# Final layer norm of a decoder step: three of nine row tiles by VectorE statistics, a ScalarE scaling pass and GpSimd products

## What is computed

```python
def layer_norm(x, g, b):
    xf = x.astype(jnp.float32)
    mu = xf.mean(-1, keepdims=True)
    var = jnp.square(xf - mu).mean(-1, keepdims=True)
    return ((xf - mu) * lax.rsqrt(var + LN_EPS) * g + b).astype(x.dtype)
...
yp = layer_norm(ALPHA * yp + moe(yp, w_router, b_router, w1[l], w3[l], w2[l]), ln2_g[l], ln2_b[l])
ys = layer_norm(ALPHA * ys + moe(ys, w_router, b_router, w1[l], w3[l], w2[l]), ln2_g[l], ln2_b[l])
```

## Time and profile before

| | us |
|---|---|
| median of 3 runs | 1405.29 (1403.64 to 1407.12) |
| the profiled execution, its own time | 1407.36 |
| its span, first to last instruction | 1405.37 |
| TensorE / VectorE / ScalarE / GpSimd busy in the span | 1286.0 / 882.7 / 577.1 / 224.2 |
| mean granted TensorE clock | 0.965 |

### The profile page before, as it was taken

How to read it: one execution, slowest core, us unless ns; L and a number is a source line. 1 busy time by engine, 2 the same in 40 slices (tenths; PEclk the granted TensorE clock), 3 DMA queues, 4 the chain that set the end, 5 groups by cost and what they waited for, 6 DMA issues and landing times.

```text
span 1405.4 us, 20304 instructions
## 1 busy us (share of the span) xinstructions
PE 1286.0 (92%) x7862; PEld 1088.6 (77%) x7862; DVE 882.7 (63%) x1416; ACT 577.1 (41%) x892; POOL 224.2 (16%) x213
## 2 busy tenths in 40 slices
PE   6999999998999999999999999999649999999940
PEld 4788667774699999999889999777538778888830
DVE  3574454434557777665332445557868899999936
ACT  3452564325621111112111111212327888888837
POOL 0200000006022212410210000000472111122130
PEclk9999999999999999999999999999759999999975
DMA  8123301002056655654563512423778999997736
GB/s 242 56 88 108 129 1 40 21 5 86 8 191 198 212 173 174 201 192 169 173 245 98 210 68 87 146 66 91 287 293 310 379 300 339 313 318 248 254 79 241
DMA packets 75428, 240.24 MB, mean 171 GB/s; under 512 B 17093, under 2 KB 27556, under 8 KB 61502
## 3 DMA queue, kind: packets, MB, share of 16 engines
q1 hardware_dynamic: 48598, 160.80, 32.3%
q0 software_dynamic: 18032, 61.31, 14.7%
q10 hardware_dynamic: 8704, 16.84, 3.4%
HBM read 215.65 MB, written 65.76 MB: 200 GB/s over the span
## 4 chain that ended last, share of the span: by engine, by line
PE 79%; DVE 4%; ACT 4%; DMA 4%; issue 2%; POOL 0%; SPq 0%; POOLq 0%; DVEq 0%; ACTq 0%
PE ps L536 19%; PE ps L538 18%; PE ps L537 18%; PE ps L1543 5%; PE ps L1567 3%; PE ps L1568 3%; PE ps L1569 3%; PE ps L1674 3%; PE ps L1714 2%; DMA b<-in_w 2%; PE ps L578 1%; DMA tmp_yd<-b,b 1%; ACT b L966 1%; ACT b L962 1%; ACT b L883 1%
## 5 line engine op out<-in xcount | busy, mean ns | idle before, releaser
L536 PE MATMUL ps<-b,b 128*128 128x344 f32 (+2 forms) x1488 | 525.6, 353 | 3.9 <-issue 2.0
L538 PE MATMUL ps<-b,b 128*128 128x344 f32 (+2 forms) x1488 | 515.6, 347 | 0.0
L537 PE MATMUL ps<-b,b 128*128 128x344 f32 (+2 forms) x1488 | 515.6, 346 | 0.0
L536 PEld LDWEIGHTS ps<-b,b 128*128 128x128 f32 (+1 forms) x1488 | 279.3, 188 | 37.7 <-issue 11.9
L538 PEld LDWEIGHTS ps<-b,b 128*128 128x128 f32 (+1 forms) x1488 | 278.9, 187 | 24.7
L537 PEld LDWEIGHTS ps<-b,b 128*128 128x128 f32 (+1 forms) x1488 | 279.2, 188 | 21.3
L813 ACT ACTIVATE b<-ps,b 128x344 f32<-128x344 f32 x96 | 52.7, 549 | 391.6 <-PE ps L538 391.6
L1315 DVE TENSOR_TENSOR b<-b,b 128x2048 fp32r<-128x2048 f32 x64 | 146.5, 2291 | 18.5 <-ACT b L883 16.4
L1543 PE MATMUL ps<-b,b 128*128 128x128 f32 (+1 forms) x782 | 116.0, 281 | 35.2 <-DMA b<-tmp_xs 18.3
L1104 DVE TENSOR_TENSOR b<-b,ps 128x344 f32<-128x344 f32 x72 | 36.9, 512 | 176.3 <-PE ps L538 169.8
L1543 PEld LDWEIGHTS ps<-b,b 128*128 128x128 f32 (+1 forms) x782 | 91.3, 144 | 60.6 <-DMA b<-tmp_xs 18.4
(11 more groups left out here) (289 smaller groups left out, 1500.5 us busy)
## 6 DMA issues: line engine op xcount, KB each, us to landing
b<-in_w SPq DMA_DIRECT2D x96, 1024.0 KB
b<-in_w_merge SPq DMA_DIRECT2D x32, 640.5 KB, 4.5
tmp_xs<-b ACTq DMA_DIRECT2D x32, 514.0 KB, 4.4
b<-tmp_xs SPq DMA_DIRECT2D x32, 514.0 KB
b<-in_w_in SPq DMA_DIRECT2D x8, 1024.0 KB, 7.5
b<-in_xT SPq DMA_DIRECT2D x4, 1024.0 KB, 11.9
b<-in_w_out SPq DMA_DIRECT2D x4, 1024.0 KB, 8.0
b<-in_x SPq DMA_DIRECT2D x8, 512.0 KB, 4.1
```

The source lines that it names most:

```text
L536: mm(out, hi, mhi, start=start, stop=False)
L537: mm(out, hi, mlo, start=False, stop=False)
L538: return mm(out, lo, mhi, start=False, stop=stop)
```

## The change

Slots 1, 3 and 5 go another way. VectorE takes their mean and variance with `bn_stats` and `bn_aggr` (`moments`), ScalarE takes the root (`root`), VectorE forms the reciprocal and minus mean times reciprocal (`shift`), ScalarE makes one pass z * reciprocal + shift in place (`scaled`), and GpSimd multiplies by the weight and adds the offset, two passes with two tensors from SBUF. The other six slots are done as before. `fs` gets a place of its own for each slot. SyncE loads slot 3 ahead of slot 2 and stores slot 6 ahead of slot 5. The order of the calls on each engine is written out.

```diff
-        fs = at(o, [P, 4, 8]); o += 128
+        fs = at(o, [P, NT + 1, 8]); o += 32 * (NT + 1)
...
+        ON_POOL = (1, 3, 5)
+        ON_DVE = tuple(s for s in range(NT + 1) if s not in ON_POOL)
+        OUT_ORDER = (0, 1, 2, 3, 4, 6, 5, 7, 8)
...
-            for s in range(NT + 1):
+            for s in (0, 1, 3, 2, 4, 5, 6, 7, 8):
                 t = WORDER[s]
                 r = rows(t)
                 sp.dma_start(acc[0:r, s, 0:D], a["yd"][t * P:t * P + r, :]).then_inc(S(f"yg{s}"), 16)
-            for s in range(NT + 1):
+            for s in OUT_ORDER:
                 t = WORDER[s]
-                sp.wait_ge(S("y_ready"), s + 1)
+                if s in ON_POOL:
+                    sp.wait_ge(S("yp"), N("yp", 2 * ON_POOL.index(s) + 2))
+                else:
+                    sp.wait_ge(S("y_ready"), ON_DVE.index(s) + 1)
...
-                if s >= 4:
-                    act.wait_ge(S("y_ready"), s - 3)
...
+            def root(s, count):
+                f = fs[:, s]
+                act.wait_ge(S("bn"), N("bn", count))
+                act.activation(f[:, 3:4], f[:, 1:2], ACT.Sqrt, bias=epsb[:]).then_inc(S("sd"), 1)
+
+            def scaled(s, count):
+                f, z = fs[:, s], acc[:, s, 0:D]
+                act.wait_ge(S("bn"), N("bn", count))
+                act.activation(z, z, ACT.Identity, scale=f[:, 4:5], bias=f[:, 2:3]).then_inc(S("aff"), 1)
+
+            row_sums(0)
+            root(1, 1)
+            squares(0)
+            root(3, 2)
+            scaled(1, 3)
+            row_sums(2)
+            squares(2)
+            scaled(3, 4)
+            row_sums(4)
+            squares(4)
+            root(5, 5)
+            row_sums(6)
+            scaled(5, 6)
+            squares(6)
+            for s in (7, 8):
+                row_sums(s)
+                squares(s)
...
+            def moments(s, count=0):
+                z = acc[:, s, 0:D]
+                if count:
+                    dve.wait_ge(S("bn"), N("bn", count))
+                dve.wait_ge(S(f"yg{s}"), 16)
+                for c in range(2):
+                    m = dve.bn_stats(st12[:, c, :], z[:, c * 512:(c + 1) * 512])
+                link(m)
+                dve.bn_aggr(fs[:, s, 0:2], st12[:].rearrange("p c s -> p (c s)")).then_inc(S("bn"), 1)
+
+            def shift(s):
+                f = fs[:, s]
+                dve.wait_ge(S("sd"), roots[s])
+                link(dve.reciprocal(f[:, 4:5], f[:, 3:4]))
+                dve.scalar_tensor_tensor(f[:, 2:3], f[:, 0:1], -1.0, f[:, 4:5], ALU.mult, ALU.mult).then_inc(S("bn"), 1)
...
-            for s in range(NT + 1):
+            moments(1)
+            moments(3, 1)
+            shift(1)
+            finish(0)
+            shift(3)
+            finish(2)
+            moments(5, 2)
+            finish(4)
+            shift(5)
+            for s in (6, 7, 8):
                 finish(s)
...
+            pool.wait_ge(S("ln2"), 32)
+            for n, s in enumerate(ON_POOL):
+                z = acc[:, s, 0:D]
+                pool.wait_ge(S("aff"), N("aff", n + 1))
+                pool.tensor_tensor(z, z, ln2[:, 0, :], ALU.mult).then_inc(S("yp"), 1)
+                pool.wait_ge(S("yp"), N("yp", 2 * n + 1))
+                pool.tensor_tensor(z, z, ln2[:, 1, :], ALU.add).then_inc(S("yp"), 1)
```

More of the change, by code:

```diff
@@ L93, in build @@
             "plg": ("po_mm", 6), "lgT": ("oDn", 6), "sel16": ("fb", 1),
+            "bn": ("macc", 72), "aff": ("dex", 2), "yp": ("v_done", 17),
             "os": ("softplus", 2), "x2": ("v_done", 1), "vo": ("lpre", 1), "heads": ("ltot", 1),
@@ L953, in emit_act2, with row_sums @@
                     h_evict(q + 1)
-            for s in range(NT + 1):
+            def row_sums(s):
                 r = rows(WORDER[s])
-                z = acc[0:r, s, 0:D]
-                f = fs[0:r, s % 4]
-                if s >= 4:
-                    act.wait_ge(S("y_ready"), s - 3)
                 act.wait_ge(S(f"yg{s}"), 16)
-                act.activation(junk[0:r, :], z, ACT.Identity, accum_out=f[:, 0:1]).then_inc(S("sums"), 1)
-                act.wait_ge(S("sums"), 3 * s + 1)
+                act.activation(junk[0:r, :], acc[0:r, s, 0:D], ACT.Identity, accum_out=fs[0:r, s, 0:1]).then_inc(S("sums"), 1)
@@ L964, in emit_act2, with squares @@
+            def squares(s):
+                r = rows(WORDER[s])
+                f, i = fs[0:r, s], 3 * ON_DVE.index(s)
+                act.wait_ge(S("sums"), i + 1)
                 act.activation(f[:, 1:2], f[:, 0:1], ACT.Copy, scale=-1.0 / D).then_inc(S("sums"), 1)
-                act.wait_ge(S("sums"), 3 * s + 2)
-                act.activation(junk[0:r, :], z, ACT.Square, bias=f[:, 1:2], accum_out=f[:, 2:3]).then_inc(S("sums"), 1)
-                act.wait_ge(S("sums"), 3 * s + 3)
+                act.wait_ge(S("sums"), i + 2)
+                act.activation(junk[0:r, :], acc[0:r, s, 0:D], ACT.Square, bias=f[:, 1:2], accum_out=f[:, 2:3]).then_inc(S("sums"), 1)
+                act.wait_ge(S("sums"), i + 3)
@@ L1381, in emit_dve2 @@
                     h_low(q + 1)
+            roots = {s: NT + 3 + n for n, s in enumerate((1, 0, 3, 2, 4, 5, 6, 7, 8))}
+            def moments(s, count=0):
[12 more added lines that the diff above has]
+                dve.scalar_tensor_tensor(f[:, 2:3], f[:, 0:1], -1.0, f[:, 4:5], ALU.mult, ALU.mult).then_inc(S("bn"), 1)
             def finish(s):
@@ L1385, in finish @@
                 z = acc[0:r, s, 0:D]
-                f = fs[0:r, s % 4]
-                dve.wait_ge(S("sd"), NT + 1 + s + 2)
+                f = fs[0:r, s]
+                dve.wait_ge(S("sd"), roots[s])
                 link(dve.reciprocal(f[:, 4:5], f[:, 3:4]))
```

## The result

The changed kernel takes 1412.38 us in the median of 7 runs (1410.0 to 1418.86), the kernel before 1405.11 beside it (1403.64 to 1408.82). The ratio is 1.0054, with an interval of 1.0032 to 1.0075: slower, by little but clear of no change. A second set of runs of both kernels, with the last experiments, gave 1.0074 (1.0056 to 1.0092). The forecast was 1412.6, in a range of 1403.6 to 1416.0.

A forecast was written before the change was run, and what follows sets the result against it. ScalarE and VectorE, both nearly full, bound the last stage. 6.0 us off, 4.85 back in waits and 8.45 of mutual GpSimd/VectorE waiting gave +7.3 on the median 1405.29: 1412.6 us, range 1403.6 to 1416.0.

The forecast's parts named there:

- What bounds the stage: Last stage: of 30.09 us ScalarE is busy 26.39, VectorE 24.57, GpSimd 0; gain must come from ScalarE without VectorE filling.
- The walk without contention: Last stage, GpSimd costing VectorE nothing: 6.0 us off, 4.85 back in new waits, stage 1.1 earlier, span 1404.2.
- The hidden table load: Ahead of ScalarE's first root: the 1.28 us load runs during the wait for VectorE, taking 1.2 us more off.
- The direction that had no row: VectorE behind a long GpSimd read: price between 0 and 2.36 us per pass; forecast took mutual whole-operation waits.
- The size: Last stage with mutual waits: 9.85 us of VectorE waiting, 8.45 on the path; span 1412.7, +7.3 us, 0.52%.
- Six places: VectorE operations held up by GpSimd, on tiles 0, 2, 3, 4 and twice on 6: 0.42 to 2.24 us each.
- The first, where only GpSimd waits: Rival, from tile 0's second pass: VectorE never waits for GpSimd; span 1404.2, -1.1 us; chance 0.21.
- The second, a partial hold: Rival: GpSimd holds the port for only part of an operation; with 1.04 us, span 1406.65, +1.3 us; chance 0.09.
- The third, a real gain: Rival: over 0.3% gain, VectorE delaying neither first root nor tile 5's pass; span 1399.4 without added waits; chance 0.03.
- The store queue does not bind: End of the stage: tile 5 is ready at 1403.0, tile 6, stored ahead of it, at 1404.2.

The follow-up runs named there:

- with fills: Changed kernel with each GpSimd pass replaced by a fill of 2048 columns of a spare array, which reads nothing; ratio to the kernel before 0.9981.
- with copies: Changed kernel with each GpSimd pass replaced by a copy of 2048 columns from one SBUF source to a spare array; ratio to the kernel before 1.0015.
- with PSUM: Changed kernel with all six GpSimd passes, but VectorE's wide passes read weight and offset from PSUM, copied there by ScalarE; ratio to the kernel before 0.9990.

## Why the prediction was right

- **What bounds the stage.** Right: the difference lies in the stage (6.0 of 6.4 us of span), and both engines' totals had to be watched together.
- **The walk without contention.** It put the work at 28.95 us (1372.25 to 1401.2); the run without GpSimd's passes measured 28.5. The hidden table load came as read from the earlier trace rows, here in the changed kernel:

```profile
1373.82 1.28 ACT L981 ACT_TABLE_LOAD   x1
1376.58 0.29 ACT L981 ACTIVATE b<-b,b 128x1 f32<-128x1 f32 x1 [1.48 <-DVE b L1429]
```

  The load ran ahead of the first root's wait for VectorE's statistics. ScalarE's scaling pass is 1.24 rather than 1.15 us, and the first statistics began 2.4 us after ScalarE's first row sum rather than 2.15; the small VectorE operations follow each other closer than was taken.
- **The direction that had no row.** The forecast's choice, that VectorE waits as GpSimd does, was the step with the largest stake, 8.4 us. Nothing in the rows of before decided it, so this was a choice between two readings, and it came out. GpSimd's product at 1380.04 held a pass begun 0.06 later until about its own end at 1382.38, and the runs with fills, with copies and with PSUM confirm it. The rule of the Trainium skill (SBUF — State Buffer, Who interferes with whom) that was set beside it says the same, and the traces agree with each part of it that they touch: two SBUF inputs (3.35 us), one SBUF input (statistics, 1.27), a GpSimd operation that only writes (1.27).
- **The size.** Six places were forecast with 9.85 us of waiting; at the same six places the operations are longer by 2.08, 1.95, 2.07, 0.50, 0.30 and 1.97, together 8.9. Where a whole pass of GpSimd was met, the forecast took 2.24 and the traces show 1.97 to 2.08, because the held pass ends 1.07 us behind GpSimd's and not 1.28. The difference between the changed kernel's work and that without GpSimd is 7.7, forecast 8.45. The walk put the work at 37.45 us (1372.25 to 1409.7), 7.4 more than before; the trace shows 36.2, 6.1 more. The medians differ by 7.3 us in the first set of runs and by 10.4 in the second, the traces by 6.0 to the end of the span and 6.4 of span. So that the forecast 1412.6 met the median 1412.38 to 0.2 us is luck; what holds is a loss of 6 to 7 us with the stated mechanism.
- **The rivals.** The first, where only GpSimd waits, needed passes of 1.28 us; five of the twelve wide passes are longer, three of them by 2 us. The second, a partial hold, needed about 1 us per GpSimd pass; a pass met at its start holds VectorE for all but 0.2 us of its 2.35. The third, a real gain, needed ScalarE not to wait for VectorE; it waited 5.0 us for factors and 3.6 for statistics. A gain, 0.1% and 0.3% in two sets of runs, took another order, fewer slots on GpSimd and weights in PSUM.
- **What was not foreseen.** Nothing in the steps spoke of the program's end. "The store queue does not bind" was right, but the engine that came within 0.5 us of binding was GpSimd, by its drain.

## What to carry to other kernels

Before elementwise work goes to GpSimd, look at what VectorE reads meanwhile: with two SBUF tensors the two engines take turns, and the work moved comes back as VectorE time. A constant operand of VectorE put into PSUM while an engine is idle removes the conflict at no cost per pass, and a one-column product of two tensors can take one of them as a number per row. Where GpSimd works near the end of a program, let it finish over 6 us ahead of VectorE's last pass, behind which the last store is issued (with 5.8 us the drain still ended last, with 6.5 it did not); in a stage that all engines share, give it the early tiles.

## What the runs showed of the hardware that was not expected

- The closing drain of GpSimd ends 8.8 us after its last operation, whether that was a product of 2.35 us (11.2 in all) or a fill of 0.10 (8.94); behind the last indirect write of the kernel before it ended 9.4 us later. The kernel without GpSimd's passes still had it, 8.81 us long, and over before the end. What it does in that time no run here shows.
- VectorE's wait for GpSimd is inside the operation's own duration (3.35 for 1.28), so the profile counts it as busy and the waits view does not list it; the sign is a duration that is no longer constant.
- A two-tensor operation of VectorE on a single column waits like a wide one, 2.11 us for 0.16.
- Reading the second tensor from PSUM costs VectorE nothing at 128x1024 in f32: 1.281 us in the median for 1.285.
